# A two-block transformer kernel: Strassen's seven products for seven pairs of gate tiles and for part of the down projection, and another form of the last gate

## Chip, core and metric

The kernel runs on one core of one Trainium2 chip. The metric is the device time of one execution in microseconds. All matrix products are of float32 data that is rounded to fp32r.

## What is computed

The reference is two transformer blocks on one sequence of 512 tokens with 1024 channels. What matters here is cut from it:

```python
gates = jax.nn.sigmoid(gm.reshape(B, S, N_BRANCH, D))
merged = gates[:, :, 0] * ua + gates[:, :, 1] * ub + gates[:, :, 2] * uc
x = x + jnp.einsum('bsd,de->bse', merged, w_o[l])
...
def conv_ffn(h, w_up, conv_w, w_down):
    gu = causal_dwconv(h @ w_up, conv_w)
    g, u = jnp.split(gu, 2, axis=-1)
    return (jax.nn.silu(g) * u) @ w_down
...
gate = jax.nn.sigmoid((x @ ple_w_gate[i]).astype(jnp.float32))
x = x + (gate * (p[i] @ ple_w_proj[i]).astype(jnp.float32)).astype(dt)
return rmsnorm(x, final_norm_gain)
```

The columns gm of the first projection make 24 gate tiles (three branches, eight tiles of 128 channels). The feed-forward layer has 2816 inner channels, 22 blocks of 128, and its down projection has eight output tiles.

## The kernel before

All activations stand transposed: 128 channels on the partitions, 512 tokens as columns. A projection tile is 128 output channels by 512 tokens in one bank of PSUM. Every float32 operand is split into a rounded part (hi) and a remainder (lo), and a product of a 128x128 weight block is three matmuls: hi x hi, hi x lo of the activation, lo of the weight x hi (L973, L974, L976).

The weights come as one stream, `wall`, cut into units of up to four blocks (128x512, 256 KB). SP loads unit u into one of five buffers `raw` (L2415) once the remainder of unit u - 5 has been written. ACT rounds it into `whi` (one of six, L1319), once TensorE is done with unit u - 6. POOL subtracts and writes `wlo` (L2315). TensorE reads both.

The order of everything is one list of steps, which `Plan.stages` and `Plan.second` write out by hand. Each engine walks this list and emits its own part of a step; an engine's instructions run in that order. `split_to` puts the split of a unit into the list five units (LOOK) ahead of the one that TensorE enters:

```python
def split_to(self, last):
    while self.split_next <= min(last, len(self.units) - 1):
        self.add("split", self.split_next)
        self.split_next += 1
```

The stages in order: the first projection with three kinds of attention (softmax on DVE and ACT in a background pipeline beside the projections); the nine gate tiles of d = 0 to 2 in that pipeline, ended by ACT's tanh (`gm_out`, L1455); three more gates for each d from 3 on, then the up products of d (4 blocks each for C, A and B), which DVE multiplies and adds (`up_out`), ACT and DVE split (`merged`, L1472); the output projection; the second block; the feed-forward up projection, 44 tiles, each followed by DVE's convolution (L1743, L1750, L1755 on zf and cv) and, per pair, tanh on ACT (L1666), a product on DVE, rounding on ACT (FH, L1671) and the remainder on POOL (FL); then the down projection, where tile d is 22 blocks in one bank and DVE adds the bank to X (`down_out`, L1746), with the rounding of X to HH (L1679) and HL for the next product. `p_in` loads p (PR), rounds it on ACT (PH, L1675) and takes the remainder on DVE (PL, L2255); it stands ahead of the down projection. Eight small tiles (p products, L1683) and the gate product follow. The last gate tiles are halves of 256 tokens, so that the final norm of the first half runs beside the product of the second. The very last gate, d = 7 of the second half, is exp on ACT (L1694), then +1 and a reciprocal on DVE (L1750, L2270); the others are tanh. The sum of squares (L1288, L1290, L1292) ends the matmuls.

## Time and profile before

| | us |
|---|---|
| median of three runs | 1239.1 (1238.69 to 1239.29) |
| the profiled execution | 1240.67 |
| its span, first to last instruction | 1238.8 |
| TensorE busy | 1220.9 |
| DVE busy | 654.3 |
| ACT busy | 550.8 |
| POOL busy | 665.4 |

The busy time of TensorE contains overlapping matmuls, so the time of one is read from the distance of two starts, not from its own length. In a timeline, "x6" merges neighbours of one kind, and the bracket at the end is the idle time of the engine before the instruction and who ended it. In the windows, PEclk is the granted clock as a share of 2.4 GHz. The time of the profiled execution lies 1.9 above its span.

### The profile page before, as it was taken

To read this page: it belongs to the slowest core of one execution; us is meant where nothing else is said; L and a number is where in the kernel's file an instruction comes from. 1 tells how busy PE (TensorE), PEld (TensorE's weight loads), DVE (VectorE), ACT (ScalarE), POOL (GpSimd) and SP (SyncE) were. 2 spreads that over 40 slices of the span, in tenths; PEclk is the share of its full clock that TensorE was granted. 3 is DMA by queue.
4 is the path that set the end of the run, shared out by engine and by line. 5 is a ranking of instruction groups with operands and counts; after the bars stand their busy time and mean duration, and the time that the engine had idled before them with its cause. 6 is when DMAs were issued, how large, how long until landed. Compare 5 with 4: busy or idle time off the path is not lost.

```text
span 1238.8 us, 17043 instructions
## 1 busy us (share of the span) xinstructions
PE 1220.9 (99%) x6262; PEld 979.3 (79%) x6262; DVE 654.3 (53%) x1103; ACT 550.8 (44%) x1077; POOL 665.4 (54%) x500
## 2 busy tenths in 40 slices
PE   9999999999999999999999999999999999999996
PEld 7977777787788888887887777788888888788885
DVE  6555427757624221144597565489999998000024
ACT  6364535676644333345644656532223322322343
POOL 8673233263356544445384566456767676655541
PEclk9999999999999999999999999999999999999998
DMA  7332222222233333353142223323333333433321
GB/s 241 102 94 75 61 64 57 60 76 70 61 85 95 101 85 102 85 162 114 52 113 63 56 62 100 100 71 87 101 102 94 86 94 98 124 94 94 102 68 69
DMA packets 62426, 112.14 MB, mean 91 GB/s; under 512 B 6856, under 2 KB 11464, under 8 KB 62344
## 3 DMA queue, kind: packets, MB, share of 16 engines
q1 hardware_dynamic: 62200, 111.06, 31.6%
q8 instruction: 50, 0.82, 0.3%
q14 instruction: 32, 0.26, 0.1%
q10 hardware_dynamic: 144, 0.00, 0.0%
HBM read 108.87 MB, written 2.16 MB: 90 GB/s over the span
## 4 chain that ended last, share of the span: by engine, by line
PE 93%; DVE 4%; issue 1%; ACT 1%; DMA 1%; POOL 1%; SPq 0%; DVEq 0%; POOLq 0%; ACTq 0%
PE pb L973 26%; PE pb L974 25%; PE pb L976 25%; PE pb L1136 2%; PE pb L1112 2%; PE pb L989 2%; PE pb L1079 1%; PE pb L1050 1%; PE pb L1052 1%; PE pb L1051 1%; PE pb L1033 1%; PE pb L1031 1%; PE pb L1101 1%; PE pb L1256 1%; DVE P L1750 1%
## 5 line engine op out<-in xcount | busy, mean ns | idle before, releaser
L2315 POOL TENSOR_TENSOR wlo<-raw,whi 128x512 fp32r<-128x512 f32 (+3 forms) x395 | 545.5, 1395 | 426.4 <-ACT whi L1319 426.1
L973 PE MATMUL pb<-HH,whi 128*128 128x512 f32 x968 | 389.7, 403 | 0.0
L974 PE MATMUL pb<-HL,whi 128*128 128x512 f32 x968 | 382.9, 396 | 0.0
L976 PE MATMUL pb<-HH,wlo 128*128 128x512 f32 x968 | 381.6, 394 | 0.0
L1319 ACT ACTIVATE whi<-raw 128x512 fp32r<-128x512 f32 (+3 forms) x395 | 234.5, 615 | 175.9 <-PE pb L976 143.0
L973 PEld LDWEIGHTS pb<-HH,whi 128*128 128x128 f32 x968 | 182.3, 188 | 47.3 <-issue 4.6
L974 PEld LDWEIGHTS pb<-HL,whi 128*128 128x128 f32 x968 | 182.1, 188 | 43.0 <-issue 2.9
L976 PEld LDWEIGHTS pb<-HH,wlo 128*128 128x128 f32 x968 | 182.0, 188 | 42.4
L1755 DVE SCALAR_TENSOR_TENSOR cv<-zf,vecs,cv 128x512 f32<-128x512 f32 x88 | 124.7, 1417 | 3.1
L1746 DVE TENSOR_TENSOR X<-pb,X 128x512 f32<-128x512 f32 x24 | 16.6, 690 | 134.2 <-PE pb L976 133.8
L1403 ACT ACTIVATE P<-P,stat 128x256 f32<-128x256 f32 (+3 forms) x96 | 50.5, 527 | 80.6 <-DVE stat L1880 58.3
L1755 DVE SCALAR_TENSOR_TENSOR gms<-gms,pb 128x512 f32<-128x512 f32 x24 | 16.4, 686 | 105.4 <-PE pb L976 105.4
L974 PE MATMUL pb<-fl,whi 128*128 128x512 f32 x176 | 69.7, 396 | 0.0
L976 PE MATMUL pb<-fh,wlo 128*128 128x512 f32 x176 | 69.4, 394 | 0.2 <-POOL wlo L2315 0.2
L973 PE MATMUL pb<-fh,whi 128*128 128x512 f32 x176 | 69.4, 394 | 0.0
L2315 POOL TENSOR_TENSOR fl<-cv,fh 128x512 fp32r<-128x512 f32 x22 | 32.3, 1468 | 63.5 <-ACT fh L1671 63.5
L1671 ACT ACTIVATE fh<-cv 128x512 fp32r<-128x512 f32 x22 | 13.9, 633 | 103.7 <-DVE cv L1755 103.7
L1755 DVE SCALAR_TENSOR_TENSOR cv<-cv,cv 128x512 f32<-128x512 f32 x44 | 35.5, 807 | 17.8 <-ACT cv L1666 15.4
L1880 DVE CUSTOM_DVE_ANT_0 P<-pb,B 128x256 f32<-128x256 f32 (+3 forms) x64 | 26.5, 436 | 34.6 <-PE pb L1101 15.6
L1666 ACT ACTIVATE cv<-cv 128x512 f32<-128x512 f32 x22 | 13.9, 633 | 67.5 <-DVE cv L1755 67.5
L976 PEld LDWEIGHTS pb<-fh,wlo 128*128 128x128 f32 x176 | 33.1, 188 | 8.3 <-POOL wlo L2315 0.6
L973 PEld LDWEIGHTS pb<-fh,whi 128*128 128x128 f32 x176 | 33.1, 188 | 8.0
(399 smaller groups left out, 1903.2 us busy)
## 6 DMA issues: line engine op xcount, KB each, us to landing
raw<-in_wall SPq DMA_DIRECT2D x368, 256.0 KB, 2.7
raw<-in_wall SPq DMA_DIRECT2D x8, 260.0 KB, 3.0
X<-in_xT SPq DMA_DIRECT2D x8, 256.0 KB, 5.1
X<-in_xT SPq DMA_DIRECT2D x2, 1024.0 KB, 8.5
outT<-PP SPq DMA_DIRECT2D x8, 256.0 KB, 2.5
raw<-in_wall SPq DMA_DIRECT2D x10, 192.0 KB, 2.4
raw<-in_wall SPq DMA_DIRECT2D x9, 128.0 KB, 2.1
cst<-in_cst SPq DMA_DIRECT2D x1, 832.0 KB, 7.8
```

The lines of the kernel that those rows point to most:

```text
L973: pe.do.matmul(b, hi, xh[k], start=start, stop=False)
L974: pe.do.matmul(b, hi, xl[k], start=False, stop=False)
L976: m = pe.do.matmul(b, lo, xh[k], start=False, stop=stop)
L989: i = pe.do.matmul(ps("kC", m), w[u % NS][:, P * m:P * m + P], x[k], start=start, stop=stop)
L1112: z = pe.do.transpose(ps(*tile)[:, o + P * j:o + P * j + P], p[:, P * j:P * j + P], ident)
L1136: z = pe.do.matmul(o, w, pt, start=j == 0, stop=j == n - 1)
L1319: a.do.activation(whi[u % NS][:, 0:n], raw[u % NR][:, 0:n], ACT.Copy).then_inc(*up("whi", ("whi", u)))
L1403: a.do.activation(p, p, ACT.Exp, bias=stat(u, 4 * m + 1), scale=-1.0, accum_out=stat(u, 4 * m + 2)).then_inc(*up("a_exp", ("exp", u, m)))
L1746: v.do.tensor_tensor(dst, x, y, ALU.add).then_inc(*up(name, *points))
L1755: v.do.scalar_tensor_tensor(out=dst, in0=x, scalar=s, in1=y, op0=op0, op1=op1).then_inc(*up(name, *points))
L1880: v.do.tensor_tensor_reduce(Pr[s % 6][:, 0:wd], ps("scores", *u, m)[:, 0:wd], bias, -1.0, -LOWEST, ALU.add, ALU.min, stat(u, 0 if kind == ...
L2315: g.do.tensor_tensor(lo, x, hi.bitcast(F32), ALU.subtract).then_inc(*up(name, point))
```

## The change

A pair is two output tiles, one and two, over eight weight blocks. Its weights are four quarters of four blocks: A11 and A12 for tile one, A21 and A22 for tile two, over the first and the last four blocks. The activations are X11, X12 (left and right 256 tokens of the first four blocks) and X21, X22. Seven products (`product7`, each 4 blocks x 3 matmuls of 256 columns) take the place of eight:

A11 with X11; A12 with X21; S4 with X22; A22 with X21 - T2; S1 with T0; S2 with T2; S3 with T1, where S1 = A21 + A22, S2 = S1 - A11, S3 = A11 - A21, S4 = A12 - S2, T0 = X12 - X11, T1 = X22 - X12, T2 = X22 - T0.

The S are 128x512 sums that DVE forms from the raw loads; they are split by ACT and POOL as a loaded unit is, but for S3, whose remainder DVE writes. The T are formed once per activation, for k = 0 to 3 (`t_sums`: DVE six instructions, ACT a rounding of 128x1024, POOL a remainder of 128x1024): four for the gates, in the first block, and four for the down projection. The gates from the eleventh on make seven pairs. There DVE and ACT add the banks into the gate tiles and ACT applies tanh. In the down projection the pairs cover blocks 0 to 7 of the 22 for tiles (0,1), (2,3), (4,5), (6,7). For the first two tiles the blocks 8 to 21 come first and the pair after, then the pair of tiles 2 and 3; the later pairs stand ahead of their tiles. Part of the products is accumulated in the tile's bank, the rest DVE adds into X. The rounding of X for the next product (`h4`) moves to the last two down tiles, and `p_in` behind the first pair. The very last gate becomes exp, ln, exp on ACT behind a bound by -44 on DVE, and nine matmuls into a spare bank stand ahead of the last matmuls.

```diff
-WARM = 8
+WARM, KEEP = 8, 9
+BRANCH = {"c": 2, "a": 0, "b": 1}
+TURN = [(d, n) for d in range(8) for n in "cab"]
+PAIRS = [tuple((d, BRANCH[n]) for d, n in TURN[i:i + 2]) for i in range(10, 24, 2)]
+NGATE = len(PAIRS)
+FACTORS = ("A11", "A22", "S2", "S1", "S3", "A12", "S4")
...
+def quarters(p):
+
+    if p < NGATE:
+        mat, (one, two) = "win", (gm_col(*x) for x in PAIRS[p])
+    else:
+        mat, one, two = "ffn_dn", 2 * P * (p - NGATE), 2 * P * (p - NGATE) + P
+    return {"A11": (mat, one, 0), "A22": (mat, two, 4), "A21": (mat, two, 0), "A12": (mat, one, 4)}
+
...
-    for d in range(8):
-        if d >= 3:
-            for j in range(3):
-                fm("win", GM + 1024 * j + P * d)
-        units.append([(n, k, P * d, P) for n in ("up_c", "up_a") for k in range(4)])
-        units.append([("up_b", k, P * d, P) for k in range(4)])
+    for i, (d, n) in enumerate(TURN):
+        if i == 9:
+            fm("win", gm_col(d, BRANCH[n]))
+        elif i >= 10 and i % 2 == 0:
+            fm4((i - 10) // 2)
...
-    for d in range(8):
-        for k in range(0, NPAIR, 8):
-            units.append([("ffn_dn", kk, P * d, P) for kk in range(k, min(k + 8, NPAIR))])
+    for q in range(4):
+        if q:
+            fm4(NGATE + q)
+        for d in (2 * q, 2 * q + 1):
+            units.append([("ffn_dn", k, P * d, P) for k in range(8, NPAIR)])
+        if q == 0:
+            fm4(NGATE)
...
+    def pair(self, p):
+
+        for i, x in enumerate("abcde"):
+            if p < NGATE:
+                self.hold(3 + i, ("acc", p, x))
+        for x in FACTORS:
+            self.split_to(self.unit_of[p, x] + LOOK)
+            self.add("product7", p, x)
...
                 gm(d, j)
+                if (d, j) == (1, 1):
+                    add("t_sums", 0, 0)
         for t in range(4):
             gate("gateA", "yA", t)
+            if t == 2:
+                add("t_sums", 0, 1)
         for t in range(4):
             gate("gateB", "yB", t)
         while self.background:
             self.step()
         add("rg_const")
-        for d in range(8):
-            if d >= 3:
-                for j in range(3):
-                    gm(d, j)
-            for n in "cab":
-                take("main", ("up", n, d))
-                self.proj(("up", n, d), "up_" + n, P * d, range(4))
-                add("up_out", n, d)
-            add("merged", d)
+        add("t_sums", 0, 2)
+        for i, (d, n) in enumerate(TURN):
+            if i == 9:
+                gm(d, BRANCH[n])
+            elif i >= 10 and i % 2 == 0:
+                self.pair((i - 10) // 2)
+            take("ups", ("up", n, d))
+            self.proj(("up", n, d), "up_" + n, P * d, range(4))
+            add("up_out", n, d)
+            if n == "b":
+                add("merged", d)
+                if d == 0:
+                    add("t_sums", 0, 3)
         add("x_again")
...
-        add("p_in")
-        for d in range(8):
-            take(("down", d))
-            self.proj(("down", d), "ffn_dn", P * d, range(NPAIR))
-            add("down_out", d)
+        for kp in range(4):
+            add("t_sums", 1, kp)
+
+        def h4(i):
+            if i % 2 and i < 12:
+                add("h4", i // 2)
+
+        for q in range(4):
+            one, two = 2 * q, 2 * q + 1
+            for i, t in enumerate((("down", one), ("down", two), ("dn", q, "ab"), ("dn", q, "cd"))):
+                self.hold(4 * (q % 2) + i, t)
+            if q:
+                self.pair(NGATE + q)
+            self.proj(("down", one), "ffn_dn", P * one, range(8, NPAIR), start=q == 0, stop=q > 0,
+                      between=h4 if q == 3 else None)
+            if q:
+                add("down_out", one)
+            self.proj(("down", two), "ffn_dn", P * two, range(8, NPAIR), start=q == 0, stop=q > 0)
+            if q == 0:
+                self.pair(NGATE)
+                add("down_out", one)
+                add("p_in")
+            add("down_out", two)
+        for d in (6, 7):
+            add("h4", d)
...
         take(("norm4", 1))
+        take(("keep",))
...
+            def product7(p, x):
+                u = plan.unit_of[p, x]
+                hi, lo = whi[u % NS], wlo[u % NS]
...
+                pe.wait_ge(*at("whi", u))
+                pe.wait_ge(*at("wlo", u))
+                for k in range(4):
+                    if x in T_AT:
+                        pe.wait_ge(*at("t_hi", g, k))
+                        pe.wait_ge(*at("t_lo", g, k))
+                        c = slice(H * T_AT[x], H * T_AT[x] + H)
+                        xh, xl = ths[k][:, c], tls[k][:, c]
...
+                    w = slice(P * k, P * k + P)
+                    begins = k == 0 and starts
+                    pe.do.matmul(b, hi[:, w], xh, start=begins, stop=False, skip_group_check=True)
+                    pe.do.matmul(b, hi[:, w], xl, start=False, stop=False, skip_group_check=True)
+                    m = pe.do.matmul(b, lo[:, w], xh, start=False, stop=k == 3, skip_group_check=True)
+                m.then_inc(*up("product", ("used", u), ("product7", p, x), *later))
...
+                if half:
+                    free(("keep",))
+                    for _ in range(KEEP):
+                        pe.do.matmul(ps("keep"), HH[:, 0:P], HH[:, 0:T], start=True, stop=True)
...
+                load, factor = units[u]
+                if load is not None:
+                    n = int(plan.offset[load + 1] - plan.offset[load])
+                    x = raw[load % NR][:, 0:n]
+                    a.wait_ge(*at("raw", load))
+                else:
+                    n, x = T, sums_at(factor[0])[factor[1]]
+                    a.wait_ge(*at("s7", *factor))
                 if u >= NS:
                     a.wait_ge(*at("used", u - NS))
-                a.do.activation(whi[u % NS][:, 0:n], raw[u % NR][:, 0:n], ACT.Copy).then_inc(*up("whi", ("whi", u)))
+                a.do.activation(whi[u % NS][:, 0:n], x, ACT.Copy).then_inc(*up("whi", ("whi", u)))
+
+            def t_sums(g, kp):
+                a.wait_ge(*at("t_raw", g, kp))
...
-                    a.do.activation(y, ps("pg", d, half)[:, 0:H], ACT.Exp, scale=-1.0).then_inc(
-                        *up("a_gate", ("pg_exp",), ("empty", ("pg", d, half))))
+                    a.wait_ge(*at("pg_bounded"))
+                    a.do.activation(y, y, ACT.Exp, scale=-1.0).then_inc(*up("a_gate"))
+                    a.wait_ge(*last("a_gate"))
+                    a.do.activation(y, y, ACT.Ln, bias=one).then_inc(*up("a_gate"))
+                    a.wait_ge(*last("a_gate"))
+                    a.do.activation(y, y, ACT.Exp, scale=-1.0).then_inc(*up("a_gate", ("pg_gate",)))
...
+                if x == "S2":
+                    for y in ("A22", "A21"):
+                        v.wait_ge(*at("raw", plan.load_of[p, y]))
+                    if p:
+                        v.wait_ge(*at("wlo", plan.unit_of[p - 1, "S4"]))
+                    weights("S1", arrived["A21"], arrived["A22"], ALU.add)
+                    v.wait_ge(*at("raw", plan.load_of[p, "A11"]))
+                    if p:
+                        v.wait_ge(*at("wlo", plan.unit_of[p - 1, "S2"]))
+                    v.wait_ge(*at("s7", p, "S1"))
+                    weights("S2", sums["S1"], arrived["A11"], ALU.subtract)
+                elif x == "S3":
+                    if p:
+                        v.wait_ge(*at("wlo", plan.unit_of[p - 1, "S3"]))
+                    weights("S3", arrived["A11"], arrived["A21"], ALU.subtract)
+                elif x == "A12":
+                    w = plan.unit_of[p, "S3"]
+                    v.wait_ge(*at("whi", w))
+                    v.do.tensor_tensor(wlo[w % NS][:, 0:T], sums["S3"], whi[w % NS][:, 0:T].bitcast(F32),
+                                       ALU.subtract).then_inc(*up("v_lo", ("wlo", w)))
+                elif x == "S4":
+                    v.wait_ge(*at("raw", plan.load_of[p, "A12"]))
+                    v.wait_ge(*at("wlo", plan.unit_of[p, "S1"]))
+                    weights("S4", arrived["A12"], sums["S2"], ALU.subtract)
...
+                if g:
+                    v.wait_ge(*at("full", ("ffn", 1, NPAIR - 1)))
...
+                for i, n in enumerate((kp, kp + 4)):
+                    v.wait_ge(*at(("x_lo", "f_lo")[g], n))
+                    v.wait_ge(*at(("x_hi", "f_hi")[g], n))
+                    step(ts[:, T * i:T * i + T], xhs[n][:, :].bitcast(F32), xls[n][:, :].bitcast(F32), ALU.add)
+                v.wait_ge(*last("v_t7"))
+                step(x11, x12, x11, ALU.subtract)
+                v.wait_ge(*last("v_t7"))
+                step(x12, x22, x12, ALU.subtract)
+                v.wait_ge(*last("v_t7"))
+                step(x22, x22, x11, ALU.subtract)
+                v.wait_ge(*last("v_t7"))
+                step(x21, x21, x22, ALU.subtract, ("t_raw", g, kp))
...
+                if x == "S2":
+                    v.wait_ge(*at("product7", p, "S2"))
+                    v.wait_ge(*last("v_c7"))
+                    v.do.tensor_copy(U7, ps("dn", q, "ab")[:, left]).then_inc(*up("v_c7"))
+                    v.wait_ge(*last("v_c7"))
+                    plus(U7, ps("dn", q, "ab")[:, right], U7)
+                    plus(x1[:, left], ps("dn", q, "ab")[:, left], x1[:, left], ("empty", ("dn", q, "ab")))
+                elif x == "S3":
+                    v.wait_ge(*at("product7", p, "S3"))
+                    v.wait_ge(*last("v_c7"))
+                    plus(W8, ps("dn", q, "cd")[:, left], U7)
+                    plus(x2[:, left], x2[:, left], U7)
+                    v.wait_ge(*last("v_c7"))
+                    plus(x1[:, right], x1[:, right], W8)
+                    plus(x2[:, right], x2[:, right], W8)
+                    v.wait_ge(*last("v_c7"))
+                    plus(x2[:, left], ps("dn", q, "cd")[:, right], x2[:, left])
+                    plus(x2[:, right], ps("dn", q, "cd")[:, right], x2[:, right], ("empty", ("dn", q, "cd")), ("sums8", q))
 
...
+                    if (d, half) == (3, 0):
+                        v.wait_ge(*at("full", ("pg", 7, 1)))
+                        affine(t4[9 % 4][:, 0:H], ps("pg", 7, 1)[:, 0:H], -44.0, None, ALU.max, None, ("pg_bounded",),
+                               ("empty", ("pg", 7, 1)), name="v_gate")
...
+                    if n >= NR:
+                        for point in freed[n - NR]:
+                            s.wait_ge(*at(*point))
```

How the instructions move is shown at three places.

ACT, from the end of the feed-forward up projection into the down projection. The names whi_54 to whi_59 are the six buffers of `whi`; whi_57 with 256 columns is the last unit of down tile 0 after the change, whi_58 the first of tile 1. Before:

```order
L1319 ACTIVATE whi_54<-raw_49 128x512
L1319 ACTIVATE whi_55<-raw_50 128x512
L1671 ACTIVATE fh_261<-cv_293 128x512
L1675 ACTIVATE PH<-PR 128x1024
L1319 ACTIVATE whi_56<-raw_51 128x256
L1319 ACTIVATE whi_57<-raw_52 128x512
```

After:

```order
L1470 ACTIVATE whi_57<-raw_49 128x256
L1470 ACTIVATE whi_58<-raw_50 128x512
L1847 ACTIVATE fh_292<-cv_324 128x512
L1474 ACTIVATE t8h_152<-t8s_160 128x1024
L1474 ACTIVATE t8h_153<-t8s_161 128x1024
L1474 ACTIVATE t8h_154<-t8s_162 128x1024
L1474 ACTIVATE t8h_155<-t8s_163 128x1024
L1470 ACTIVATE whi_59<-raw_51 128x512
L1470 ACTIVATE whi_54<-raw_52 128x512
```

Four roundings of the activation sums (t8h from t8s) now stand between the last rounding of the feed-forward product and the split of the second unit of tile 1; the rounding of p is gone from there.

DVE, in the first two down pairs, after the change (u_168 and w_170 hold sums of banks, s7a, s7b and s8c the weight sums):

```order
L1969 TENSOR_TENSOR s7b<-s7a,raw_53 128x512
L2056 TENSOR_TENSOR w_170<-pb,u_168 128x256
L2056 TENSOR_TENSOR X<-X,u_168 128x256
L2056 TENSOR_TENSOR X<-X,w_170 128x256 x2
L2056 TENSOR_TENSOR X<-pb,X 128x256 x2
L1969 TENSOR_TENSOR s8c<-raw_53,raw_50 128x512
L1929 TENSOR_TENSOR X<-pb,X 128x512
L2554 TENSOR_TENSOR PL<-PR,PH 128x1024
L1929 TENSOR_TENSOR X<-pb,X 128x512
L1989 TENSOR_TENSOR wlo_61<-s8c,whi_55 128x512
```

The remainder of p (PL), which before stood directly behind the last convolution, now stands between S3 of the second pair (s8c) and that S3's remainder (wlo_61).

DVE at the end of the kernel. Before:

```order
L1743 TENSOR_TENSOR PP<-PP,pb 128x256 x3
L1755 SCALAR_TENSOR_TENSOR PP<-X,vecs,pb 128x256 x2
L1750 TENSOR_SCALAR t_299<-t_299 128x256
L2270 RECIPROCAL t_299<-t_299 128x256
L1743 TENSOR_TENSOR t_299<-t_299,PP 128x256
```

After:

```order
L1926 TENSOR_TENSOR PP<-PP,pb 128x256 x2
L1933 TENSOR_SCALAR t_330<-pb 128x256
L1926 TENSOR_TENSOR PP<-PP,pb 128x256
L1938 SCALAR_TENSOR_TENSOR PP<-X,vecs,pb 128x256 x2
L1926 TENSOR_TENSOR t_330<-t_330,PP 128x256
```

The bound stands after two of the three multiplies of the first half, and the +1 and the reciprocal are gone.

## Rows read from the trace of the kernel before

**Rows 1.** The page, part 1: busy us (share of the span) xinstructions

```profile
PE 1220.9 (99%) x6262; PEld 979.3 (79%) x6262; DVE 654.3 (53%) x1103; ACT 550.8 (44%) x1077; POOL 665.4 (54%) x500
```

**Rows 2.** Windows: gates with up products, feed-forward up, last matmuls

```profile
core 0: us, PE busy (x) PEld busy (x) DVE busy (x) ACT busy (x) POOL busy (x), PEclk, DMA share, GB/s
391.00:534.20 143.20, 143.20 (x618) 115.97 (x617) 33.16 (x46) 43.45 (x75) 71.08 (x54) 1.00 0.34 96
804.00:1045.00 241.00, 241.00 (x1037) 194.64 (x1035) 215.53 (x214) 73.14 (x130) 161.24 (x105) 1.00 0.33 91
...
1230.00:1232.00 2.00, 1.18 (x2) 0.50 (x2) 0.73 (x2) 0.00 (x0) 0.00 (x0) 0.50 0.08 28
```

**Rows 3.** Timeline of TensorE, down tile 0: start us, length us

```profile
1045.00 0.39 PE L973 MATMUL pb<-fh,whi 128*128 128x512 f32 x1
...
1057.56 0.40 PE L973 MATMUL pb<-fh,whi 128*128 128x512 f32 x1
...
1059.76 0.50 PE L976 MATMUL pb<-fh,wlo 128*128 128x512 f32 x1 [0.18 <-POOL wlo L2315]
```

**Rows 4.** Timeline of TensorE, half tiles of 256 columns, every 24th matmul

```profile
1212.84 0.28 PE L1278 MATMUL pb<-HH,whi 128*128 128x256 f32 x1
...
1215.63 0.28 PE L1278 MATMUL pb<-HH,whi 128*128 128x256 f32 x1
...
1218.44 0.28 PE L1278 MATMUL pb<-HH,whi 128*128 128x256 f32 x1
```

**Rows 5.** Groups by line and form: their weight loads, busy us, mean ns

```profile
L1278 PEld LDWEIGHTS pb<-HH,whi 128*128 128x128 f32 x32 | 6.0, 188 | 0.1
```

**Rows 6.** Timeline of all engines at the end of the kernel

```profile
1224.97 1.08 DVE L1743 TENSOR_TENSOR PP<-PP,pb 128x256 f32<-128x256 f32 x3 [2.25 <-ACT pb L1725]
...
1226.76 0.84 DVE L1750 TENSOR_SCALAR t<-t 128x256 f32<-128x256 f32 x1
1227.63 1.75 DVE L2270 RECIPROCAL t<-t 128x256 f32<-128x256 f32 x1
1229.42 0.43 DVE L1743 TENSOR_TENSOR t<-t,PP 128x256 f32<-128x256 f32 x1
1229.88 0.43 DVE L1746 TENSOR_TENSOR X<-t,X 128x256 f32<-128x256 f32 x1
...
1230.82 1.22 PE L1292 MATMUL pb<-sq,cst 128*128 128x256 f32 x2 [4.46 <-DVE sq L1743]
...
1232.59 0.39 ACT L1725 ACTIVATE pb<-rs 128x256 f32<-128x256 f32 x1
```

**Rows 7.** Timeline of TensorE at the start of the kernel

```profile
1.45 3.78 PE L983 MATMUL pb<-HH 128*128 128x512 f32 x8 [1.45 <-DVE HH L1759]
5.13 1.78 PE L989 MATMUL pb<-MH,whi 128*128 128x512 f32 x4
```

**Rows 8.** Timeline of the other engines, around the start of the down projection

```profile
1050.56 0.69 DVE L1755 SCALAR_TENSOR_TENSOR cv<-cv,cv 128x512 f32<-128x512 f32 x1
1051.29 0.63 ACT L1671 ACTIVATE fh<-cv 128x512 fp32r<-128x512 f32 x1 [4.79 <-DVE cv L1755]
1051.99 1.29 POOL L2315 TENSOR_TENSOR fl<-cv,fh 128x512 fp32r<-128x512 f32 x1 [2.88 <-ACT fh L1671]
1053.37 0.38 SPq L2458 DMA_DIRECT2D PR<-in_pT  x1
1056.71 1.06 ACT L1675 ACTIVATE PH<-PR 128x1024 fp32r<-128x1024 f32 x1 [4.79 <-DMA PR<-in_pT]
...
1057.88 1.23 DVE L2255 TENSOR_TENSOR PL<-PR,PH 128x1024 fp32r<-128x1024 f32 x1 [6.62 <-ACT PH L1675]
```

**Rows 9.** Line L1755, convolution: ns min/median/max, first and last start us

```profile
L1755 DVE SCALAR_TENSOR_TENSOR cv<-zf,vecs,cv x88: 750/1660/1680, 808.1 to 1049.7; 128x512 f32<-128x512 f32 x88
```

**Rows 10.** Tile gms, additions of the gated products, the same columns

```profile
L1746 DVE TENSOR_TENSOR gms<-gms,gms x16: 691/692/1740, 392.3 to 535.6; 128x512 f32<-128x512 f32 x16
```

**Rows 11.** Timeline of POOL in the feed-forward up projection

```profile
1042.51 3.44 POOL L2315 TENSOR_TENSOR wlo<-raw,whi 128x512 fp32r<-128x512 f32 x2
```

**Rows 12.** Timeline of DVE in the softmax beside the first gates

```profile
315.19 0.42 DVE L1880 CUSTOM_DVE_ANT_0 P<-pb,B 128x256 f32<-128x256 f32 x1 [3.01 <-PE pb L1079]
```

237 lines of the change are left out of this document (195 added, 42 removed).

## The prediction

> **What bounds the kernel now.** I read the page's busy times first, then windows by stage, then TensorE's timeline at the places that the change touches, then the waits of ACT, DVE and POOL there. TensorE is busy for 1220.9 of 1238.8 us [rows 1]; in the window of the last gates and up products and in that of the feed-forward up products it has no gap at all, at full clock [rows 2]. So work that leaves TensorE is worth its whole time, and a wait that reaches TensorE costs its whole time. POOL is busy for half of the gate window, DVE for nearly all of the feed-forward window. The profiled execution took 1240.67 us (span 1238.8 and 1.9 around it), 1.6 over the median of 1239.1; the sum below is a difference, and I add it to the median. A measurement of this kernel can tell about 0.2%, 2.5 us, from no change.
>
> **Matmul time removed.** Before, a pair of tiles over eight weight blocks is 2 x 8 x 3 = 48 matmuls of 512 columns. Now it is 7 products x 4 blocks x 3 = 84 of 256 columns, each with weights of its own. From the first matmul of the down projection (1045.00) to the first of its 19th block (1057.56) are 54 matmuls: 0.2326 us each [rows 3]. The 256-column half tiles start 24 matmuls in 2.79 and 2.81 us, 0.1167 each [rows 4]. So 48 x 0.2326 = 11.16 becomes 84 x 0.1167 = 9.80, and 11 pairs (seven of gates, four of down) give **-14.9 us**. The weight load of these matmuls, 0.188 us each [rows 5], is longer than the interval and did not stretch it. The Trainium skill ("TensorE: Matmul & The Clock Gate", the section on packing small matmuls) says that a weight load overlaps a running matmul only in other row groups; by that rule a product would take at least 0.188 us per matmul and the pairs would lose time. The trace disagrees, and the sum goes by the trace.
>
> **The last gate.** Before, DVE does a +1 (0.84) and a reciprocal (1.75) behind ACT's exp and behind its own outputs of the first half, and the final sum of squares starts at 1230.82 after 4.46 us of idle TensorE [rows 6]. Now DVE puts the bound by -44 after two of its three first-half multiplies: 1224.97 + 2 x 0.36 = 1225.7, done at 1226.1; three ACT steps of 0.39 [rows 6] with 0.05 between end at 1227.5; multiply, add and square at intervals of 0.46 end at 1228.9. That is 1.9 earlier. The two last matmuls took 1.22 us at the lower clock (granted clock 0.50, half of 2.4 GHz, [rows 2]); nine matmuls of 512 columns fill 2.1 us of the gap, and at 2.4 GHz the pair takes half, 0.6 less. Together **-2.5 us**; not below -1.5 if the clock falls all the same.
>
> **The sums for the down projection, and who stands behind them.** This is the largest term. DVE must form four sums of the activations for k = 0 to 3 (each two 512-column adds and four dependent 256-column steps), ACT rounds each (128x1024), POOL takes the rest. In ACT's order these four roundings stand in front of the split of the second unit of down tile 1; the order excerpts show it. ACT and POOL take their work in order, so that unit waits for the fourth sum even though it needs none of it.
> 1. Only five units were split ahead: tile 0 (14 blocks) and 4 blocks of tile 1. Counted from E = 1045.00, TensorE reaches the 19th block at E+12.6 and the matmul with wlo at E+13.0 [rows 3].
> 2. DVE ends its last convolution at 1051.25, E+6.25 [rows 8]. One sum is 2 x 0.72 + 4 x 0.46 = 3.28 (0.69 for 512 columns [rows 10], interval 0.46 for 256 [rows 6]); four are 13.1, so E+19.4 if nothing disturbs.
> 3. POOL disturbs: it runs the last fl (1.29) and three 1024-column remainders (2.6 each, as two of 1.29) meanwhile, seven operations of 512. DVE operations with two SBUF inputs rise from 0.75 to 1.66, and from 0.69 to 1.74, beside POOL [rows 9, 10], 1.0 us per POOL operation: +7.0, E+26.4.
> 4. ACT's rounding 1.06 and a hop of 0.1 (E+27.6), POOL's fourth remainder 2.6 and the unit's wlo 1.29 (E+31.5). TensorE was due at E+13.0: a stall of **18.5 us**. The lower end, undisturbed, is 19.4 + 1.2 + 2.6 + 1.3 - 13.0 = 11.5; the upper, with POOL's last three operations of 512 at 1.72 [rows 11], 19.8.
> The kernel before shows this very line in small: ACT waits for PR until 1056.71, the splits follow, and TensorE's L976 at 1059.76 waits for wlo [rows 3, 8]. The Trainium skill ("SBUF — State Buffer", "Who interferes with whom") calls the pair that DVE and POOL share an exclusive lock, kept for the whole instruction; by it a 1024-column POOL operation would block DVE for all of its time, and the stall would be about 20.5.
> After so long an idle stretch TensorE returns at 1.2 GHz. At the kernel's start eight matmuls took 3.78 us, about 0.47 each, and the next four 1.78 [rows 7] until it ran at 2.4 GHz: about 4 us at half rate, **+2.0 us** (0 if the clock holds, 3 at most).
>
> **The input p.** Its load moves behind the first down pair, and on SP behind the loads that wait for S3 of the second pair. Let t be 0 at the first product of pair one. Its S3 ends at 7.0; DVE's six 256-column adds end near 10.1, S3 of the next pair at 10.8; SP issues PR, which took 3.34 us from issue to ACT's start [rows 8]: 14.4; PH 1.06, PL 1.23 and an add 0.69: 17.6. Only then does DVE write the remainder of S3 (0.69): 18.4. TensorE needs it at 9.8 + 5.6 = 15.4. **+3.0 us** (2 to 5). The two pairs stand back to back with no plain tile between them, so nothing covers it.
>
> **What I cost small.** In the gate stage the sums come beside slack: ACT's splits run up to five units ahead, 14 us of TensorE. Only the first lies in the softmax pipeline, where DVE has 3.0 us of idle time per step [rows 12]; 3.3 to 5 us there give +1.0 (0 to 3). A gate pair with its two up tiles takes 9.8 + 5.6 = 15.4 us. POOL has eight splits in it, 10.4 to 13.8 us (1.3 to 1.72 each [rows 11]); DVE has five operations of 512 and six of 256 beside the 3.5 us of gates and merging, 10 to 14 us. Both fit. The tightest piece is the remainder of S3 behind merging, ready near 3.8 and needed at 5.6: +0.3 (0 to 5 over seven pairs). The h4 copies move to down tiles 6 and 7; the eight p products behind them (8 x 1.4 = 11 us) hide them: 0. Loads stay 256 KB and as many: 0.
>
> **Sum**: -14.9 - 2.5 + 18.5 + 2.0 + 3.0 + 1.0 + 0.3 = +7.4, so 1239.1 + 7.4 = **1246.5 us**.
>
> **Rivals.** (a) *The sums meet no POOL work.* Place: DVE from E+6.25. Then the stall is 11.5, p costs its lower 2.0, the softmax nothing: -17.4 + 11.5 + 2.0 + 2.0 = -1.9, 1237.2. It decides where the fourth sum is written before about E+21. For it: gms additions beside POOL took 0.69 in most cases [rows 10]. Against it: each POOL remainder is released by the sum before and so lands on the next sum. Chance 0.18; a third of it is faster by over 2.5 us. (b) *The gate pairs starve as well*, each by 1.0 to 1.5 us at the remainder of S3 or at S4 (sum, rounding and remainder in series, 2.6 us or more with 8.4 to do it in), since DVE and POOL are both near full: +7 to +10, 1255. For it: 10 to 14 us of 15.4 on both engines; against it: every step there has 1.7 us or more to spare. Chance 0.10. (c) *The 256-column products are bound by their weight loads*, 0.188 each: 84 x 0.188 = 15.8 in place of 9.8, +66 in 11 pairs on the forecast, some 1312. The intervals of the half tiles speak against it [rows 4]. Chance 0.02. (d) *The change does not do what it says*: the kept-up matmuls leave the clock low, +0.6, inside the other cases.
> The forecast keeps 0.70.
>
> **How the numbers follow.** Bounds: the forecast with a stall of 14.5 and p at 2.0 gives about 1241.5; with 19.8, the clock at 3, p at 5 and the softmax at 3 it gives 1252.8. To leave out no more than 2 in 10 the range takes most of (a) and the lower part of (b): 1237.5 to 1254. Faster: a third of (a) and a little of the forecast's tail, 0.08. Same: the rest of (a), 0.12. Slower: 0.80.
>
> **What would show it.** In the profile after: the 256-column products at 0.117 us; one idle stretch of TensorE of 15 to 20 us some 12.5 us into the down projection, ended by POOL's wlo, with ACT's split waiting behind L1474 and that behind DVE's L2001; DVE's adds at L2001 longer than 0.72 where POOL runs; half clock behind the gap; a second wait of about 3 us in the second pair's S3 for DVE's L1989; the final two matmuls at 0.6. Wrong if TensorE runs through the down projection, if the sums finish within 13 us, or if the pairs of gates show waits of their own.

## The result, and the profile after

The change makes the kernel slower: 1259.4 us (median of 4 runs, 1257.3 to 1261.0) against 1238.9 (4 runs, 1238.6 to 1239.3), a ratio of 1.0165, 95% interval 1.0153 to 1.0177. That is 20.5 us more; the prediction said 7.4 more (1246.5) and a range up to 1254.0. The profiled execution took 1257.3 us, span 1255.5.

The page of the kernel after, busy times and granted clock in 40 slices (answers to [rows 1]):

```profile
PE 1214.2 (97%) x6667; PEld 994.5 (79%) x6667; DVE 791.3 (63%) x1283; ACT 580.7 (46%) x1134; POOL 724.9 (58%) x530
...
PEclk9999999999999999999999999999999998889999
```

TensorE is busy for 6.7 us less than before, and the kernel is longer: what the pairs save is more than eaten by waits, and the clock row dips in three slices, which all lie in the down projection. The waits of TensorE in the kernel after, longest first (us in total, times, longest); before there was none of these four but a wait of 0.18 us for POOL's `wlo` [rows 3]:

```profile
PE pb L1068 <- ACT whi L1470: 14.6, 1, 14.6
PE pb L1121 <- DVE wlo L1989: 6.7, 1, 6.7
PE pb L1068 <- DVE gms L1938: 4.3, 2, 2.6
PE pb L1071 <- POOL wlo L2616: 1.9, 1, 1.9
```

Windows of the kernel after: the seven gate pairs with their up products, then four places in the down projection.

```profile
core 0: us, PE busy (x) PEld busy (x) DVE busy (x) ACT busy (x) POOL busy (x), PEclk, DMA share, GB/s
422.83:531.16 108.33, 108.33 (x758) 100.94 (x756) 74.94 (x101) 49.34 (x96) 80.88 (x58) 1.00 0.37 109
1054.00:1069.00 15.00, 0.39 (x2) 0.20 (x2) 12.76 (x16) 3.94 (x5) 6.52 (x4) 0.68 0.00 0
1069.00:1073.00 4.00, 2.08 (x5) 1.17 (x6) 0.00 (x0) 1.62 (x4) 4.00 (x3) 0.50 0.02 5
1073.00:1077.00 4.00, 4.00 (x12) 3.14 (x11) 2.16 (x2) 0.00 (x0) 3.74 (x4) 0.56 0.61 192
1100.00:1105.00 5.00, 2.11 (x10) 2.14 (x11) 4.43 (x7) 1.85 (x5) 2.67 (x2) 0.54 0.11 19
```

In the pairs of gates TensorE has no gap and runs at full clock, so the matmuls do what was forecast of them. In the down projection three stretches have gaps or matmuls at 1.2 GHz (PEclk 0.50 to 0.56). From TensorE's timeline, the stages before and after, in the two profiled executions:

| stretch | before | after | difference |
|---|---|---|---|
| up products of d = 0 to 2 (108 matmuls) | 25.11 | 31.27 | +6.2 |
| gate pair (48 matmuls of 512; 84 of 256), each of seven | 11.15 | 9.90 | -1.25, in all -8.8 |
| down pair, each of four, without its waits | 11.20 | 9.80 | -1.4, in all -5.6 |
| plain blocks of down tiles 0 and 1 (84 matmuls) | 19.6 | 39.17 | +19.6 |
| pairs 0 and 1 of the down projection (168 matmuls) | 19.6 (at 9.80) | 28.53 | +8.9 |
| first of the last two sums (L1288, L1429) to the end of the span | 13.5 | 11.1 | -2.4 |

Together +17.9, and what lies between (-0.9 in the softmax pipeline, -0.4 elsewhere) makes it +16.6, the difference of the two profiled executions. The other 3.9 us of the medians' 20.5 are not in these traces: the one before is 1.8 over its median, the one after 2.1 under its own. More on that below, at e7.

**The hold-up in the down projection.** All engines' timelines of the kernel after, the rows that make the chain (E, the end of the feed-forward product, is 1041.46):

```profile
1047.51 1.29 DVE L2001 TENSOR_TENSOR t8s<-fh,fl 128x512 f32<-128x512 f32 x2
...
1061.89 1.28 DVE L2001 TENSOR_TENSOR t8s<-fh,fl 128x512 f32<-128x512 f32 x2
...
1063.14 2.34 POOL L2616 TENSOR_TENSOR t8l<-t8s,t8h 128x1024 fp32r<-128x1024 f32 x1 [2.83 <-ACT t8h L1474]
...
1063.21 3.93 DVE L2001 TENSOR_TENSOR t8s<-t8s 128x256 f32<-128x256 f32 x4
...
1067.18 1.06 ACT L1474 ACTIVATE t8h<-t8s 128x1024 fp32r<-128x1024 f32 x1 [4.11 <-DVE t8s L2001]
...
1068.14 2.48 ACT L1470 ACTIVATE whi<-raw 128x512 fp32r<-128x512 f32 x5
...
1068.31 2.36 POOL L2616 TENSOR_TENSOR t8l<-t8s,t8h 128x1024 fp32r<-128x1024 f32 x1 [2.83 <-ACT t8h L1474]
...
1068.80 0.80 PE L1068 MATMUL pb<-fh,whi 128*128 128x512 f32 x1 [14.61 <-ACT whi L1470]
...
1070.63 2.50 POOL L2616 TENSOR_TENSOR wlo<-raw,whi 128x512 fp32r<-128x512 f32 x2
...
1071.94 0.80 PE L1071 MATMUL pb<-fh,wlo 128*128 128x512 f32 x1 [1.92 <-POOL wlo L2616]
```

TensorE issued its last matmul before the gap at 1053.79, E+12.3. DVE started the sums at E+6.05 and wrote the fourth at 1067.14, E+25.7. ACT, which has its four roundings in front of the split, waits for each and begins five splits in a row at 1068.14. Only then does TensorE get its `whi` (14.61 us idle), and its `wlo` only behind POOL's fourth remainder. The four 256-column steps of a sum take 3.93 us here. Of the 19.6 us that this stage is longer, 16.5 are idle time and the rest are matmuls at the lower clock.

**The up products.** The same, around the third and fourth sum of x:

```profile
393.62 1.28 DVE L1938 SCALAR_TENSOR_TENSOR gms<-gms,pb 128x512 f32<-128x512 f32 x2
...
393.73 1.06 ACT L1474 ACTIVATE t7h<-t7s 128x1024 fp32r<-128x1024 f32 x1 [3.87 <-DVE t7s L2001]
...
394.35 0.79 PE L1068 MATMUL pb<-yChi,whi 128*128 128x512 f32 x1 [2.60 <-DVE gms L1938]
...
394.86 2.38 POOL L2616 TENSOR_TENSOR t7l<-t7s,t7h 128x1024 fp32r<-128x1024 f32 x1 [6.86 <-ACT t7h L1474]
...
394.93 2.87 DVE L1929 TENSOR_TENSOR gms<-gms,gms 128x512 f32<-128x512 f32 x1
...
403.54 1.80 DVE L2001 TENSOR_TENSOR t7s<-t7s 128x256 f32<-128x256 f32 x4
405.27 1.28 DVE L1938 SCALAR_TENSOR_TENSOR gms<-gms,pb 128x512 f32<-128x512 f32 x2
...
406.00 0.50 PE L1068 MATMUL pb<-yChi,whi 128*128 128x512 f32 x1 [1.71 <-DVE gms L1938]
```

Both of TensorE's waits end with a product of DVE that reads a bank and so frees it (L1938, at 393.62 and 405.27), and each of these stands directly behind a sum of x. In front of the third sum DVE still has its small steps for the second block, 4.7 us from 385.90 to 390.6, which the kernel before has there too. Between the two products lies the merging: DVE's addition of gms takes 2.87 us beside a POOL remainder of 2.38 (0.69 in the median of [rows 10], 1.74 for this same addition before). It frees no bank, but it makes everything behind it later, the fourth sum and the second product too. The granted clock there:

```profile
390.00:395.00 5.00, 2.40 (x10) 1.66 (x9) 4.72 (x13) 1.27 (x2) 0.14 (x1) 0.88 0.00 0
395.00:400.00 5.00, 5.00 (x19) 4.00 (x18) 4.46 (x3) 1.82 (x4) 5.00 (x3) 0.78 0.02 2
405.00:410.00 5.00, 4.00 (x17) 3.29 (x18) 4.97 (x5) 2.62 (x4) 3.48 (x2) 1.00 0.00 0
```

The matmuls at the lower clock lie between the two waits and make the second one shorter; DVE alone sets its end. In the traces of e6 and e7, whose program is the same up to here, the clock is full between the waits, the second is 3.06 and 3.04 us long instead of 1.71, and it ends at the same time (405.90 and 405.92; 406.00 here). So all 6.2 us of this stage are DVE's lateness.

**The input p.** SP issues the load 13.2 us after the first product of pair 0 (1080.63):

```profile
1093.82 0.39 SPq L2786 DMA_DIRECT2D PR<-in_pT  x1
...
1098.65 1.06 ACT L1851 ACTIVATE PH<-PR 128x1024 fp32r<-128x1024 f32 x1 [5.14 <-DMA PR<-in_pT]
...
1099.81 1.23 DVE L2554 TENSOR_TENSOR PL<-PR,PH 128x1024 fp32r<-128x1024 f32 x1 [6.36 <-ACT PH L1851]
...
1101.55 1.19 DVE L1989 TENSOR_TENSOR wlo<-s8c,whi 128x512 fp32r<-128x512 f32 x1
...
1102.89 0.55 PE L1121 MATMUL pb<-t8h,whi 128*128 128x256 f32 x1 [6.68 <-DVE wlo L1989]
```

TensorE's wait of 6.68 us ends 0.15 us after DVE's remainder of S3, which stood behind PL, which waited for PH, which waited for the load. The window 1100 to 1105 above has the clock at 0.54.

**The last gate.**

```profile
1245.13 2.44 PE L1435 MATMUL pb<-HH 128*128 128x512 f32 x9
...
1248.03 0.70 PE L1437 MATMUL pb<-sq,cst 128*128 128x256 f32 x2 [0.46 <-DVE sq L1926]
```

The nine matmuls into the spare bank end, TensorE waits 0.46 us more for DVE's square, and the last two matmuls take 0.70 us at full clock. They start 3.58 us behind the first matmul of the last sums (1244.45), where it was 5.48 before (1225.34 to 1230.82, the latter in [rows 6]).

### The profile page after: what moved, and what is told of

The parts are those of the page before. It is cut to its first block, busy times and chain, and to the rows that moved or that the text cites. A ratio compares the mean times of both kernels' runs of the same rounds, so it can differ in the third digit from the quotient of the medians.

```text
span 1255.5 us, 18288 instructions
## 1 busy us (share of the span) xinstructions
PE 1214.2 (97%) x6667; PEld 994.5 (79%) x6667; DVE 791.3 (63%) x1283; ACT 580.7 (46%) x1134; POOL 724.9 (58%) x530
## 4 chain that ended last, share of the span: by engine, by line
PE 87%; DVE 8%; ACT 2%; issue 1%; DMA 1%; POOL 1%; SPq 0%; DVEq 0%; ACTq 0%; POOLq 0%
PE pb L1068 21%; PE pb L1069 21%; PE pb L1071 21%; PE pb L1121 3%; PE pb L1123 3%; PE pb L1122 3%; PE pb L1277 2%; PE pb L1253 2%; PE pb L1130 2%; DVE t8s L2001 2%; PE pb L1220 1%; PE pb L1191 1%; PE pb L1193 1%; PE pb L1192 1%; DVE cv L1938 1%
## 5 line engine op out<-in xcount | busy, mean ns | idle before, releaser
L2616 POOL TENSOR_TENSOR wlo<-raw,whi 128x512 fp32r<-128x512 f32 (+2 forms) x384 | 542.6, 1431 | 338.4 <-ACT whi L1470 337.6
L1068 PE MATMUL pb<-HH,whi 128*128 128x512 f32 x856 | 345.7, 404 | 0.0
L1069 PE MATMUL pb<-HL,whi 128*128 128x512 f32 x856 | 338.6, 396 | 0.0
L1071 PE MATMUL pb<-HH,wlo 128*128 128x512 f32 x856 | 337.6, 394 | 0.0
L1470 ACT ACTIVATE whi<-raw 128x512 fp32r<-128x512 f32 (+2 forms) x384 | 225.8, 614 | 112.1 <-PE pb L1071 64.8
L1938 DVE SCALAR_TENSOR_TENSOR cv<-zf,vecs,cv 128x512 f32<-128x512 f32 x88 | 123.8, 1407 | 3.1
L2616 POOL TENSOR_TENSOR fl<-cv,fh 128x512 fp32r<-128x512 f32 x22 | 32.6, 1482 | 64.3 <-ACT fh L1847 64.3
L1929 DVE TENSOR_TENSOR X<-pb,X 128x512 f32<-128x512 f32 x24 | 16.6, 690 | 77.0 <-PE pb L1071 76.6
L1068 PE MATMUL pb<-fh,whi 128*128 128x512 f32 x112 | 45.3, 405 | 14.6 <-ACT whi L1470 14.6
L1071 PE MATMUL pb<-fh,wlo 128*128 128x512 f32 x112 | 45.3, 404 | 1.9 <-POOL wlo L2616 1.9
L1938 DVE SCALAR_TENSOR_TENSOR cv<-cv,cv 128x512 f32<-128x512 f32 x44 | 35.6, 808 | 18.2 <-ACT cv L1842 15.4
L1069 PE MATMUL pb<-fl,whi 128*128 128x512 f32 x112 | 45.3, 404 | 0.0
L2179 DVE CUSTOM_DVE_ANT_0 P<-pb,cst 128x128 f32<-128x128 f32 (+3 forms) x32 | 14.4, 489 | 39.6 <-PE pb L1229 29.2
L1068 PE MATMUL pb<-MH,whi 128*128 128x512 f32 x96 | 38.6, 402 | 0.0
L2616 POOL TENSOR_TENSOR wlo<-s7a,whi 128x512 fp32r<-128x512 f32 x22 | 29.5, 1341 | 15.2 <-ACT whi L1470 15.0
```

Source lines behind the costliest of these rows:

```text
L1068: pe.do.matmul(b, hi, xh[k], start=start, stop=False, skip_group_check=tile[0] == "down")
L1069: pe.do.matmul(b, hi, xl[k], start=False, stop=False, skip_group_check=tile[0] == "down")
L1071: m = pe.do.matmul(b, lo, xh[k], start=False, stop=stop, skip_group_check=tile[0] == "down")
L1470: a.do.activation(whi[u % NS][:, 0:n], x, ACT.Copy).then_inc(*up("whi", ("whi", u)))
L1938: v.do.scalar_tensor_tensor(out=dst, in0=x, scalar=s, in1=y, op0=op0, op1=op1).then_inc(*up(name, *points))
L2179: v.do.tensor_tensor_reduce(Pr[s % 6][:, 0:wd], ps("scores", *u, m)[:, 0:wd], bias, -1.0, -LOWEST, ALU.add, ALU.min, stat(u, 0 if kind == ...
```

## The experiments

E is the end of the feed-forward product throughout. The last column is against 1259.4 for the change, taken as differences to the kernel before on the same chip. The 95% interval of a row against before is 1 to 2 us to either side, so two rows that lie less than some 2 us apart are not told apart by their times.

| run | us | against before | against the change |
|---|---|---|---|
| e1 gates only | 1235.3 | -4.2 | -24.7 |
| e2 tail only | 1236.8 | -2.7 | |
| e3 p later | 1248.8 | +9.4 | -11.1 |
| e4 eight banks | 1259.2 | +19.8 | -0.7 |
| e5 roundings behind tile 1 | 1257.4 | +18.7 | -1.8 |
| e6 sums spread | 1240.8 | +2.1 | -18.4 |
| e7 kept hot | 1258.9 | +20.1 | -0.4 |
| e8 eight banks, late roundings | 1258.4 | +19.7 | -0.8 |
| e9 remainders by DVE | 1251.8 | +13.1 | -7.4 |
| e10 recombined | 1226.6 | -12.1 | -32.6 |
| e11 four tiles first | 1224.3 | -14.5 | -35.0 |
| e12 new gate, nothing kept up | 1236.5 | -2.2 | |
| e13 small steps moved | 1254.3 | +15.2 | -5.3 |
| e14 moved, banks, late roundings | 1255.5 | +16.4 | -4.1 |
| e15 DVE's remainders, banks, late roundings | 1256.6 | +17.6 | -2.9 |

**e1: the gate pairs alone.** The plan and the steps of the down projection are those of before.

```diff
-        for kp in range(4):
-            add("t_sums", 1, kp)
...
+        add("p_in")
+        for d in range(8):
+            take(("down", d))
+            self.proj(("down", d), "ffn_dn", P * d, range(NPAIR))
+            add("down_out", d)
+            add("h4", d)
```

> The change with the down projection of before: seven gate pairs, the sums of x for them and the new last gate stay. Theory (the traces): of the 20.5 us lost, the down projection holds +22.7 in the profiled execution, so without its pairs the kernel is faster than before: gate pairs -8.8, softmax -0.9, up products of the first tiles +6.2, tail -2.4, together about -6, 1233. Rival (the prediction's sum, which held the sums in the gate stage beside slack): -9.5 -2.5 +1.3, 1228. Second rival: DVE and POOL, loaded by the gate pairs, also lengthen what follows (output projection, second block): 1239 or more.

Measured 1235.3 (ratio 0.9971, interval 0.9959 to 0.9983). That is 24.7 us less than the change, so the net loss lies in the down projection. The up products of d = 0 to 2 take 31.28 us here too, and so the prediction's sum for this stage (1228) is out. Nothing behind it became longer.

**e2 and e12: the last gate, with and without the nine matmuls,** on the kernel before.

```diff
+                if half:
+                    free(("keep",))
+                    for _ in range(KEEP):
+                        pe.do.matmul(ps("keep"), HH[:, 0:P], HH[:, 0:T], start=True, stop=True)
```

These lines are in e2 and not in e12; both have the exp, ln, exp of the change.

> The kernel before with the new last gate and the nine kept-up matmuls only. Theory: -2.4 (profile of after: final squares done 1.9 earlier, 0.5 less behind them), 1236.5. Rival: the gain in the profile comes from the end of the stage before (the h4 copies lie elsewhere), and the new gate alone gives under 1 us: 1238.

> The kernel before with the new last gate alone, without the nine kept-up matmuls. Theory: these are worth 0.6 us (the two last matmuls take 1.22 us at 1.2 GHz), so e2's 1236.8 becomes 1237.4. Rival: the wait of TensorE is now so short (3.6 us) that the clock stays up without them, and nothing changes: 1236.8.

Measured 1236.8 (0.998, 0.9971 to 0.9989) and 1236.5 (0.9982, 0.9972 to 0.9991). TensorE's last matmuls in e12:

```profile
1227.39 0.70 PE L1292 MATMUL pb<-sq,cst 128*128 128x256 f32 x2 [2.57 <-DVE sq L1748]
```

The two take 0.70 us, full clock, after 2.57 us of idle time; before, after 4.46 us, they took 1.22 [rows 6]. In the trace of e2 they take 0.70 too. So behind the shorter wait the clock is kept without the nine matmuls, and these are worth nothing that can be measured: the two runs differ by 0.5 us against before, inside their intervals.

**e3: ACT's and DVE's work on p behind down tile 2.** A step of its own (`p_load`) keeps SP's load where it was.

```diff
-                add("p_in")
+                add("p_load")
...
             if q:
                 add("down_out", one)
+            if q == 1:
+                add("p_in")
```

> The change, with ACT's and DVE's work on the input p behind down tile 2 in place of behind the first down pair (SP issues the load where it did). Theory: the wait of TensorE for the remainder of S3 in the second pair (6.7 us in the trace) is the wait of ACT and DVE for p; it goes, and with it the low clock behind it: 8.7 less than the change, about 1250.7. Rival 1: only the wait goes and the low clock is of another cause: 1252.7. Rival 2: DVE's six adds behind the first pair bind as much: at most 3 less, 1256.5.

Measured 11 us less than the change (8.3 in the two profiled executions), and the 168 matmuls of pairs 0 and 1 take 19.60 us, without a wait. The load is issued at the same point, 13.2 us after the first product of pair 0 (1094.41, 1081.21). The first theory holds. The low clock behind the wait goes with it.

**e4, e8, e13, e14, e15: the up products.** e4 gives the first ten of them eight banks. e8 also puts ACT's rounding and POOL's remainder of `t_sums(0,2)` and `(0,3)` later; e15 also lets DVE write these remainders; e13 moves only `rg_const`, small steps for the second block; e14 is e8 with that move.

```diff
-            take("ups", ("up", n, d))
+            take("ups" if i > 9 else "wide", ("up", n, d))
```
```diff
         for i, (d, n) in enumerate(TURN):
+            if i in (4, 7):
+                add("t_round", 0, 2 if i == 4 else 3)
```
```diff
-        add("rg_const")
...
             add("wo_out", d)
+            if d == 3:
+                add("rg_const")
```

> The change, with eight PSUM banks in place of three for the up products of the first ten turns. Theory: the 6.2 us more in that stretch (two waits for DVE's gms addition, 4.3 us, and a low clock behind them) come from DVE's delay by the sums t_sums(0,2) and (0,3), which three banks can't cover and eight can: 6.2 less, about 1253.2. Rival: DVE has no slack to catch up before the first gate pair, and the delay shows there: less than 3 us gained, 1257 or more.

> As e4 (eight banks for the first ten up products), and with it ACT's roundings of t_sums(0,2) and (0,3) four turns behind DVE's sums, so that ACT's splits of the up products stand in front of them. Theory: in e4 ACT waited 3.9 and 5.2 us for DVE's sums in front of splits, and TensorE 1.3 and 2.8 us for POOL's remainders of these splits; with both gone the 6.2 us go: 1253.2. Rival: DVE itself (sums of 3.1 and 4.2 us, behind 4.7 us of small steps for the second block) is too late for the first gate pair: 1257 or more.

> The change, with only the small steps for the second block (4.7 us on DVE with its waits for ACT) moved from in front of the up products to the middle of the output projection. Theory A (DVE is short of time as such): DVE begins the third sum 4.7 us earlier and the two waits for its gms addition (4.3 us) and the low clock go: 1253.5. Theory B (POOL's remainders block DVE, the place does not matter): the sums still stand in front of the splits and of the merging, and at most 2 us are gained: 1257.5 or more.

> e8 (eight banks, later roundings) with the small steps moved as well; POOL keeps the remainders. Theory A: all 6.2 us go, 1253. Theory B: DVE still loses 2.4 to 5 us to POOL's remainders, so a wait of 1 to 3 us is left: 1255 or more.

> e8 with the remainders of the last two sums by DVE, the small steps where they are. Theory A: DVE is still 4.7 us late; the wait of 3.8 us in e8 shrinks by no more than 1 us: 1257.5. Theory B: each remainder by DVE costs it 1.4 in place of 2.4 or more; 3 us and more are gained: 1255.

In e4 the wait only changed its name. ACT and TensorE there:

```profile
405.58 1.06 ACT L1474 ACTIVATE t7h<-t7s 128x1024 fp32r<-128x1024 f32 x1 [5.21 <-DVE t7s L2001]
...
410.82 0.80 PE L1071 MATMUL pb<-exB,wlo 128*128 128x512 f32 x1 [2.81 <-POOL wlo L2616]
```

ACT stood 5.21 us in front of its splits, and TensorE then missed a `wlo` in place of a bank. The length from the first up product to the end of the first gate pair (108 + 24 + 12 + 84 matmuls; without waits 25.11 + 5.56 + 2.80 + 9.90 = 43.4), from TensorE's timeline:

| | up, d = 0 to 2 | gate 9 | up | first pair | over 43.4 |
|---|---|---|---|---|---|
| the change | 31.27 | 5.56 | 2.80 | 9.90 | 6.2 |
| e4 | 31.86 | 6.37 | 2.79 | 9.90 | 7.6 |
| e8 | 29.07 | 7.24 | 2.79 | 10.37 | 6.1 |
| e13 | 27.60 | 5.56 | 2.79 | 9.90 | 2.5 |
| e14 | 25.12 | 5.68 | 2.79 | 13.49 | 3.7 |
| e15 | 27.00 | 5.67 | 2.79 | 14.24 | 6.3 |
| e10 | 25.11 | 5.56 | 2.79 | 10.74 | 0.8 |

Some of the last column is the lower clock behind the last of the waits. TensorE's idle time alone is 4.1 in e4, 4.0 in e8, 2.2 in e13, 1.8 in e14, 4.3 in e15 and 0.6 in e10; in the change all 6.2 are DVE's, as said above.

Banks and roundings move the lateness from the up products into the gate tile and the first pair. They cover some 2 us of it, but then the clock falls behind the last wait and takes the same back, so that nothing is won. What helps is an earlier DVE: 3.7 us by moving the small steps alone (theory A for e13), and, with them moved, 2.9 more by DVE's own remainders (e14 to e10; 1.2 of it idle time, the rest the clock, which stays full in e10). With POOL's remainders 3.7 us are left in e14, so there theory B is right. In e15 the trace shows nothing gained (6.3), though its time is 2 us under that of e8 against before, no clear difference; neither theory is borne out to the number, and DVE's remainders are not enough by themselves.

**e5: the roundings behind the splits of tile 1.**

```diff
             if q == 0:
+                for kp in range(4):
+                    add("t_round", 1, kp)
                 self.pair(NGATE)
```

> The change, with ACT's four roundings (and POOL's four remainders) of the sums for the down projection behind the splits of down tile 1, DVE's sums where they are. Theory: the hold-up of 19.6 us (16.5 idle, 3 at low clock) comes from the place of the roundings in ACT's order, in front of splits that need none of it. TensorE then runs through both plain tiles to E+19.6 and one product of the first pair (E+21), and waits there only for the last sums, rounded and with their remainder near E+29: 8 us and some 2 of low clock. About 9.5 less than the change, 1250. Rival: what decides is when DVE ends the sums (E+25.7), wherever the roundings stand, and the wait only moves from tile 1 to the first pair: 1257 or more.

My theory fell: only 2 us less. Tiles 0 and 1 now take 19.56 us, so the hold-up there is gone as said, but pairs 0 and 1 take 46.4 in place of 28.5. ACT and DVE in e5:

```profile
1062.60 1.29 DVE L2007 TENSOR_TENSOR t8s<-fh,fl 128x512 f32<-128x512 f32 x2
...
1063.93 1.80 DVE L2007 TENSOR_TENSOR t8s<-t8s 128x256 f32<-128x256 f32 x4
...
1065.64 0.68 DVE L1975 TENSOR_TENSOR s7a<-raw,raw 128x512 f32<-128x512 f32 x1
...
1067.16 0.63 ACT L1476 ACTIVATE whi<-s7b 128x512 fp32r<-128x512 f32 x1 [14.61 <-DVE s7b L1975]
...
1068.73 3.88 ACT L1480 ACTIVATE t8h<-t8s 128x1024 fp32r<-128x1024 f32 x4
```

The splits of pair 0's S2, S1 and S3 were in front of the roundings in ACT's order, and they wait for DVE, whose weight sums (s7a at 1065.64) stand behind all four sums of the activations. ACT waited 14.61 us there (by chance the same length as TensorE's wait in the change), and the roundings and POOL's remainders came one after the other behind it. The place of one step in one queue was not the whole cause: DVE's queue has the same fault. One row is worth keeping: where POOL has nothing to do, the four 256-column steps of a sum take 1.80 us.

**e6: the sums spread over three plain tiles.**

```diff
+SCHED = [("t", 0), ("t", 1), ("t", 2), ("P", 0), ("t", 3), ("P", 1), ("t", 4), ("P", 2), ("t", 5), ("P", 3), ("t", 6), ("t", 7)]
...
+        extra = {(1, 1): [('t_round', 1, 0)], (1, 8): [('t_round', 1, 1)], (2, 2): [('t_round', 1, 2)], (2, 9): [('t_round', 1, 3)], (1, 2): [('p_load',)], (4, 3): [('p_in',)]}
```

> The change, with the down projection in another order: plain tiles 0, 1, 2, then pair 0, tile 3, pair 1, tile 4, pair 2, tile 5, pair 3, tiles 6, 7; each rounding of the sums stands behind the splits that are due before it (blocks 15, 22, 30, 37), and the work on p behind tile 3. Theory: neither the hold-up in tile 1 (19.6) nor the wait for p (8.7) is left: 28.3 less than the change, 1231. Rival: DVE and POOL, which share their access, are late as such with four sums and the splits, and a wait of several us appears in front of pair 0: 1236 or more.

Between the two: 18.4 less than the change, 10 more than the theory. Plain tiles 0 to 2 run through (29.32 us), p costs nothing, but in pair 0 TensorE still waits, once for 8.5 us, and the pair takes 21.55 us in place of 9.8:

```profile
PE pb L1132 <- POOL t8l L2627: 9.1, 2, 8.5
```

Now POOL splits weights all the time that DVE sums, and the four sums take 27.5 us (1048.98 to 1076.50) where they took 19.6 in the change. The rival is right in that.

**e7: filler matmuls in the hold-up.** Sixty matmuls into a spare bank, in front of the block at which TensorE stops.

```diff
+            def hot():
+                free(("hot",))
+                for _ in range(60):
+                    m = pe.do.matmul(ps("hot"), FH[0][:, 0:P], FH[0], start=True, stop=True)
+                m.then_inc(*up("product", ("empty", ("hot",))))
```

> The change, with 60 matmuls of 512 columns (14 us of TensorE) that nobody reads, put in front of the block at which TensorE stops in down tile 1. They fill most of the idle stretch of 14.6 us and should keep the clock. Theory: of the 19.6 us, some 3 are matmuls at 1.2 GHz behind the wait; these go: 1256.4. Rival: the low clock comes from the second, short wait for POOL's remainder and from what follows, and stays: 1259.4.

The rival is right. Windows of e7 over the fillers, the two short waits and what follows:

```profile
1055.00:1070.00 15.00, 14.25 (x63) 11.45 (x61) 13.37 (x16) 3.34 (x4) 6.50 (x4) 1.00 0.01 1
1070.00:1074.00 4.00, 1.17 (x3) 0.74 (x4) 0.00 (x0) 2.23 (x5) 4.00 (x3) 0.75 0.00 0
1074.00:1079.00 5.00, 5.00 (x13) 3.84 (x13) 2.77 (x3) 0.05 (x1) 4.37 (x4) 0.52 0.54 157
```

The clock is full to 1070, falls at the second wait (2.41 us, for POOL's `wlo`), and is at 1.2 GHz for most of 1074 to 1079 all the same. Tiles 0 and 1 with the fillers take 39.6 us, no less than in the change (39.17). And in the up products, where e7 equals the change, e7 has full clock (1.00) in the windows 390 to 395 and 395 to 400, behind a wait of 2.61 us; the change has 0.88 and 0.78 there, behind one of 2.60. The window 405 to 410 of e7 reads

```profile
405.00:410.00 5.00, 4.08 (x11) 3.22 (x12) 4.93 (x6) 2.62 (x4) 3.56 (x2) 0.66 0.00 0
```

behind its second wait of 3.04 us, where the change has 1.00 behind 1.71. So the same program, behind the same wait, loses the clock in one execution and keeps it in another. It matters where: in e7 the up products of d = 0 to 2 take 32.82 us, 1.5 more than in the change. This may be part of the 2.1 us by which the profiled execution of the change lies under its median, and of the wider spread of its runs (3.7 us, before 0.7); it wasn't shown. The other 1.8 of the 3.9 us lie on the side of the kernel before.

**e9: DVE writes the remainders of the sums for the down projection itself,** behind the four sums.

```diff
+            def t_low(i, kp):
+                v.wait_ge(*at("t_hi", i, kp))
+                v.do.tensor_tensor((TL7, TL8)[i][kp], (TS7, TS8)[i][kp], (TH7, TH8)[i][kp].bitcast(F32),
+                                   ALU.subtract).then_inc(*up("v_lo", ("t_lo", i, kp)))
```

> The change, with the four 1024-column remainders of the sums for the down projection done by DVE, behind its four sums, in place of POOL. Theory: the sums take 5.2 us each, not 3.1, because each POOL remainder (2.35 us) keeps DVE from its 256-column step for all its length; in e5, where POOL had nothing to do, three sums took 3.1. Without them the fourth sum is written at about E+20 (25.7 in the change), POOL's remainder of the waiting unit no longer stands behind one of 2.4, and TensorE resumes near E+23: the hold-up shrinks by 7 to 8 us, to 1252. Rival: the long steps have another cause (their own dependence, the rounding by ACT) and stay; DVE then has 5.5 us more to do and nothing is gained: 1258 or more.

Measured 7.4 less than the change, as the theory has it. DVE and TensorE in e9:

```profile
1058.35 1.29 DVE L2003 TENSOR_TENSOR t8s<-fh,fl 128x512 f32<-128x512 f32 x2
...
1059.67 1.80 DVE L2003 TENSOR_TENSOR t8s<-t8s 128x256 f32<-128x256 f32 x4
...
1061.39 6.79 DVE L2055 TENSOR_TENSOR t8l<-t8s,t8h 128x1024 fp32r<-128x1024 f32 x4
...
1063.14 0.80 PE L1070 MATMUL pb<-fh,whi 128*128 128x512 f32 x1 [8.21 <-ACT whi L1472]
```

A sum takes 3.05 us but for the first (5.2 in the change). The fourth is written at 1061.5, E+19.3, and TensorE's wait for `whi` is 8.21 us, not 14.61. Tiles 0 and 1 take 31.07, 8.1 less; 2.3 are given back in pairs 0 and 1 (30.86), where the wait for DVE's remainder of S3 grows to 8.5 us. The four remainders take DVE 6.8 us beside POOL's splits; in e10, beside an idle POOL, one takes 1.21 us.

**e10 and e11: the remedies together.** e10 has the order of e6, e9's remainders for all sums but the first two, e8's banks and late roundings and e13's move. e11 also puts tile 3 in front of pair 0 and moves the roundings and the work on p with it. In the list of steps "t" is a plain tile and "P" a pair.

```diff
-SCHED = [("t", 0), ("t", 1), ("t", 2), ("P", 0), ("t", 3), ("P", 1), ("t", 4), ("P", 2), ("t", 5), ("P", 3), ("t", 6), ("t", 7)]
+SCHED = [("t", 0), ("t", 1), ("t", 2), ("t", 3), ("P", 0), ("P", 1), ("t", 4), ("P", 2), ("t", 5), ("P", 3), ("t", 6), ("t", 7)]
```

> All remedies together: the order of e6 for the down projection, its remainders by DVE as in e9, roundings at blocks 15, 20, 25 and 30; in the gate stage eight banks for the first ten up products, roundings and (DVE's) remainders of t_sums(0,2) and (0,3) behind the splits that are due earlier, and the 4.7 us of small steps for the second block moved from in front of the up products to the middle of the output projection. Theory: all three losses go (19.6, 8.7, and 4 to 6 of 6.2), so 1259.4 - 33 = 1226, about 1% faster than before. Rival: DVE and POOL are short as such in the stretches with sums, and some 5 us stay in each: 1236.

> As e10, with tile 3 in front of the first pair as well (plain tiles 0 to 3, pairs 0 and 1, tile 4, ...), the roundings of the sums at blocks 18, 27, 33 and 39, and the work on p behind tile 4. Theory: what is left in e10 is a wait of 2.8 us inside the first pair: its splits of S2, S1 and S3 stand behind four sums and four remainders on DVE, which end 1.2 us before they are needed. 9.8 us more of plain blocks cover that: 1223.5. Two pairs then stand back to back as in the change, and since p is not between them nothing waits. Rival: the wait in the change's second pair was also that of two pairs back to back, and comes back: 1227 or more.

Measured 1226.6 (ratio 0.9905, 0.989 to 0.9919) and 1224.3 (0.9882, 0.9867 to 0.9896). e10, windows around pair 0, where TensorE waited 2.76 us for the split of a sum:

```profile
1065.00:1070.00 5.00, 3.39 (x27) 3.09 (x25) 4.43 (x6) 1.03 (x2) 0.26 (x1) 1.00 0.00 0
1070.00:1075.00 5.00, 3.82 (x30) 3.67 (x31) 3.05 (x4) 1.63 (x4) 3.94 (x3) 1.00 0.41 131
```

The clock stays at 1.00 behind that wait. In e11 the whole down projection is one window:

```profile
1036.30:1154.36 118.06, 117.56 (x674) 102.49 (x672) 82.96 (x98) 44.34 (x76) 86.99 (x66) 1.00 0.39 109
```

118.1 us, with 0.5 of waits; it was 123.2 before and 145.9 in the change. Pairs 0 and 1 stand back to back in it and lose 0.7, so the rival of e11, that two pairs in a row starve, is out. Both kernels compute all of the output; e11 is 14.5 us faster than the kernel before and 35 faster than the change.

## Why the prediction was wrong

The direction was right, the size was not: +20.5 where +7.4 was forecast, 5.4 beyond the end of the range. Step by step:

- **Matmul time removed: -14.9 forecast, -14.4 in the traces.** The intervals are 0.1166 us in the down pairs and 0.1179 in the gate pairs (9.90 / 84). The weight loads did not bound them; rival (c) is out. So is the rule that the Trainium skill gives for packing small matmuls ("TensorE: Matmul & The Clock Gate", Part 3), that a weight load overlaps a running matmul only in other row groups: the intervals are shorter than the 0.188 us of a load. The prediction left out that the same section also lets a load run ahead into a background weight buffer, which would fit these intervals.
- **The last gate: -2.5 forecast, -2.4 in the trace, -2.7 and -2.2 by e2 and e12.** The time is right. The reason given for 0.6 of it is wrong: the clock was not kept by the nine matmuls (e12), but behind the shorter wait without them.
- **The sums for the down projection: +18.5 and +2.0 forecast, +19.6 in the trace** (16.5 idle, 3.1 at the lower clock). The chain, its order and its times are those of the prediction: fourth sum at E+26.4 forecast and E+25.7 measured, POOL's `wlo` for the waiting unit under way from E+29.2. The price of contention, 1.0 us per POOL operation of 512, was right: steps of 1.80 became 3.93 beside a remainder of 2.34. Rival (a) is out. The Trainium skill ("SBUF — State Buffer", "Who interferes with whom") calls the pair an exclusive lock for the whole instruction; the 2.1 us that 2.34 us of POOL cost DVE agree with it, and e9 takes the lock's cost away by giving the work to DVE.
- **The input p: +3.0 forecast (2 to 5), +8.9 in the trace, 11 by e3.** This step was mis-sized. The mechanism is right, to each engine of the chain. DVE wrote S3 of the second pair at t+12.2 where the sum had 10.8, the load was issued at t+13.2 where it had about 11.1 (14.4 less 3.34), and ACT began 4.8 us after the issue where 3.34 was taken. With t+22.3 for the next matmul that is 6.7 us of waiting in place of 3. The other 2 and more are matmuls at half clock behind it, which the step left out: the prediction gave the clock to the long stall only.
- **"In the gate stage the sums come beside slack": 0 beside the +1.0 for the softmax, +6.2 in the trace.** This step failed. It looked at ACT's lead of five units and not at DVE, where the third and fourth sum meet 4.7 us of small steps, the merging of the up products, and two POOL remainders that each hold up an addition (2.87 and 2.90 us). DVE's product that frees TensorE's bank came at 405.27, some 6 us too late. Moving the small steps gave 3.7 us back (e13), DVE's own remainders most of the rest (e14 to e10); more banks and later roundings gave none (e4, e8), and DVE's remainders without the move none either (e15). In the softmax pipeline, which had the +1.0, the trace shows 0.9 less than before. Rival (b), starving gate pairs at +7 to +10, named a stage next to this one; the pairs themselves ran without a gap.
- **Gate pairs +0.3, h4 and loads 0:** as forecast.

So of the 13 us missed, the traces hold 9.2: 6.2 in the gate stage and 5.9 at p with its clock, 0.6 at the matmul time and the last gate, less 0.9 at the sums for the down projection, 1.9 at the softmax, 0.3 at the gate pairs and 0.4 that is not assigned. The other 3.9 are the distances of the two profiled executions from the medians, and their cause stays open.

## What to carry to other kernels

When work is added for engines that serve TensorE in order, follow each one's queue, DVE's as well as ACT's, and put every step where its input will be ready: the same products with the sums spread, rounded late and finished by DVE, the small steps moved and p later turned +20.5 us into -14.5. A remainder of 1024 columns on POOL cost DVE 2.1 us of its own time; done by DVE it took 1.2 us (e10) or 1.7 beside POOL's splits (e9), so handing it to POOL saved DVE nothing. Price the low clock as possible behind short waits of TensorE too (it fell behind one of 1.80 us in e14), not only behind long ones. It costs only where no later wait absorbs it.

## What the runs showed of the hardware

A wait of TensorE of about 2.6 us was followed by a lower granted clock in some places and not in others: 2.60 us up to 394.35 in the change (PEclk 0.88, then 0.78) and 2.41 in e7 (0.52), but 2.61 at the same place of e7 (1.00), 2.76 in e10 (1.00) and 2.57 in e12 (1.00). In e14 a wait of 1.80 us in the first gate pair was followed by 0.79 (window 420 to 425). Length alone does not tell, and what else does was not tried. DVE's four 256-column steps took 1.80 us beside an idle POOL (e5, e9) and 3.93 beside one POOL operation of 2.34.
